# Opening, convolution end and MLP seams of a two-block transformer kernel, written in another order

## The reference, cut to what matters

```python
def first_block(x, ...):
    h = rmsnorm(x, norm1_g)
    u = h @ cc_w_in + cc_b_in                      # 2048 -> 4096
    val, gate = split(u)
    u = val * sigmoid(gate)
    u = causal_dwconv(u, cc_dw) + cc_dw_b          # 31 taps for each channel
    u = silu(layernorm(u, cc_ln_g, cc_ln_b))
    x = x + u @ cc_w_out + cc_b_out
    x = x + square(relu(rmsnorm(x, norm2_g) @ mlp_w1)) @ mlp_w2    # 2048 -> 8192 -> 2048
    return rmsnorm(x, final_g)

def second_block(x, ...):
    proj = x @ w_in                                # then pooling, sparse attention, w_out, layer norm
    ...                                            # then 128 chosen experts for each token, layer norm
```

## Time and profile before

| | |
|---|---|
| time, median of 3 runs | 2882.6 us (2881.51 to 2890.96) |
| the profiled execution: its time | 2899.03 us |
| its span, first to last instruction | 2897.1 us |
| PE busy | 2207.9 us, 76% |
| DVE busy | 1942.5 us, 67% |
| POOL busy | 2035.0 us, 70% |
| ACT busy | 1161.9 us, 40% |
| PE's mean granted clock | 0.874 of full |

### The profile page before, as it was taken

One profiled execution on the slowest core, in us unless ns is written; L12 is line 12 of the kernel. 1 busy time (PEld: TensorE's weight loads), 2 busy tenths in 40 slices (PEclk: granted clock), 3 DMA queues, 4 the chain that ended last, 5 costly groups with the idle time before them and its releaser, 6 DMA issues. The chain is left out here.

```text
span 2897.1 us, 40891 instructions
## 1 busy us (share of the span) xinstructions
PE 2207.9 (76%) x12632; PEld 1946.7 (67%) x12632; DVE 1942.5 (67%) x3016; ACT 1161.9 (40%) x1888; POOL 2035.0 (70%) x1140
## 2 busy tenths in 40 slices
PE   6998999999999999999989700002330289999996
PEld 5997788888888888999978600002220278878785
DVE  2997322624426223464445999999999888888888
ACT  4343545454454544333430100008970254444443
POOL 3773688888888877577751566787878537777774
PEclk9999999999999999999999955555555699999998
DMA  5552455555555555364434999999999649999997
GB/s 182 168 173 87 145 189 181 189 181 190 187 188 183 179 172 186 117 204 147 159 132 149 416 368 381 392 413 377 410 409 401 242 159 337 329 321 326 317 317 253
DMA packets 231978, 713.75 MB, mean 246 GB/s; under 512 B 17418, under 2 KB 53826, under 8 KB 198722
## 3 DMA queue, kind: packets, MB, share of 16 engines
q1 hardware_dynamic: 168512, 364.08, 37.3%
q0 software_dynamic: 57344, 343.97, 30.5%
q10 hardware_dynamic: 6048, 4.81, 0.5%
HBM read 709.12 MB, written 3.67 MB: 246 GB/s over the span
## 5 line engine op out<-in xcount | busy, mean ns | idle before, releaser
L381 POOL TENSOR_TENSOR w_lo<-raw,w_hi 128x1024 fp32r<-128x1024 f32 x464 | 1125.5, 2443 | 368.1 <-ACT w_hi L815 366.4
L815 ACT CAST w_hi<-raw 128x1024 fp32r<-128x1024 f32 x464 | 482.9, 1050 | 671.8 <-PE bank L460 411.1
L458 PE MATMUL bank<-B,w_hi 128*128 128x512 f32 x1280 | 457.4, 402 | 15.4 <-DVE B L1210 8.7
L458 PE MATMUL bank<-A,w_hi 128*128 128x512 f32 x1280 | 452.7, 399 | 0.0
L421 POOL DMA_INDIRECT vrows<-in_peer_v,vring x256 | 327.0, 1277 | 146.7 <-POOL vring L415 104.3
L1330 DVE TENSOR_TENSOR sq<-bank,T 128x256 f32<-128x256 f32 x128 | 54.2, 425 | 459.3 <-ACT T L942 458.9
L460 PE MATMUL bank<-B,w_lo 128*128 128x256 f32 x1280 | 361.3, 282 | 0.0
L460 PE MATMUL bank<-A,w_lo 128*128 128x256 f32 x1280 | 359.5, 281 | 0.0
L397 POOL DMA_INDIRECT rows_split<-in_peer_u,ering x128 | 253.3, 1979 | 134.5 <-DVE dots L1573 82.1
L463 PE MATMUL bank<-A,w_hi 128*128 128x256 f32 x1152 | 333.3, 289 | 5.6 <-DVE proj L1374 2.9
L464 PE MATMUL bank<-A,w_hi 128*128 128x256 f32 x1152 | 329.8, 286 | 0.0
(11 more groups left out here) (243 smaller groups left out, 4529.6 us busy)
## 6 DMA issues: line engine op xcount, KB each, us to landing
raw<-in_mlp_w SPq DMA_DIRECT2D x128, 1024.0 KB, 5.1
v_raw<-in_peer_v SPq DMA_DIRECT2D x128, 736.0 KB, 6.3
raw<-in_w_in SPq DMA_DIRECT2D x40, 1024.0 KB, 5.0
raw<-in_cc_w_in SPq DMA_DIRECT2D x64, 512.0 KB, 4.8
raw<-in_cc_w_out SPq DMA_DIRECT2D x16, 1024.0 KB, 5.0
raw<-in_w_out SPq DMA_DIRECT2D x16, 1024.0 KB, 5.1
raw<-in_peer_wq SPq DMA_DIRECT2D x16, 1024.0 KB, 5.1
vrows<-in_peer_v,vring POOLq DMA_INDIRECT x256, 6.2
```

Of the source, the lines that this page charges most:

```text
L381: nc.gpsimd.tensor_tensor(w_lo[:, s % 4], raw[:, s // 2, 2 * (s % 2):2 * (s % 2) + 2, :], w_hi[:, s % 4].bitcast(F32), ALU.subtract).then_ ...
L458: nc.tensor.matmul(bank[m][:].rearrange("p (s t) -> p s t", s=2), wh, both[:, :, kt, :], start=(kt == 0), stop=False)
L815: nc.scalar.copy(w_hi[:, s % 4], raw[:, s // 2, 2 * (s % 2):2 * (s % 2) + 2, :]).then_inc(hi_done, 1)
```

## The change

Six edits, none of which changes what is computed:

1. The depthwise taps are fetched as 124 rows of 512 numbers instead of 31 rows of 2048, to another place, so that VectorE's clearing of `dwn` goes. TensorE turns them with 4 instead of 16 instructions.
2. The squares of x are divided: ScalarE takes tokens 0 to 127 and VectorE tokens 128 to 255 by `tensor_tensor_reduce`. `xsc` is made in four halves.
3. TensorE turns x itself first, as it arrives, into eight PSUM banks, and ScalarE copies `X` right after `VT`. The turns of `xsc` come behind it. ScalarE's cast of step 2 of group 0 comes after two `A_hi` instead of before all.
4. In the last convolution group the diagonals are written between the casts, and the sigmoids stand right behind the casts.
5. One-column activations (`load_table`) load a function table ahead of its use at six places.
6. In `G_OUT` and in the MLP's last four groups ScalarE casts steps 3 to 6 of the next group before its RMS tiles (`four_more`). The mean of squares ahead of the second layer is made before step 7 instead of step 5.

```diff
-        dwn = at("dwn", o_x, [32, D])
+        dwn = at("dwn", o_z + 56 * KB, [P, D // 4])
...
@@ block.tensor
             def turn_taps():
...
-                for k in range(KT):
-                    last = nc.tensor.transpose(misc[3][:, 32 * k:32 * k + 32], dwn[:, k * P:(k + 1) * P], ident[0:32, 0:32])
+                for b in range(4):
+                    last = nc.tensor.transpose(misc[3][:, 4 * TAPS * b:4 * TAPS * (b + 1)], dwn[0:4 * TAPS, b * P:(b + 1) * P],
+                                               ident[0:4 * TAPS, 0:4 * TAPS])
...
-            pe.wait_ge(xsc_ok, 2)
-            to_channels(xsc, x_ps, n_out["rms1"], 2)
+            for r in range(KT // 2):
+                pe.wait_ge(part_in[r // 2], 16)
+                if r == 7:
+                    pe.wait_ge(vt_ok, 1)
+                to_channels(xnat, r, x_banks[r])
+            for r in range(KT // 2):
+                pe.wait_ge(xsc_ok, 2 if r < 4 else 4)
+                if r < 4:
+                    pe.wait_ge(x_ok, r + 1)
+                else:
+                    pe.wait_ge(n_out["rms1"], 2 * (r - 3))
+                to_channels(xsc, r, misc[r % 4])
...
             groups(A_hi, A_lo, G_IN, 1, n_op["rms1"], order=swap, hooks={6: turn_taps})
             pe.wait_ge(vt_ok, 2)
-            to_channels(xnat, x_ps, x_ok, 1)
...
-            project(0, {5: lambda: mean_of_sum(ssq_ok, 2 * KT, n_mean["rms3"])})
+            project(0, {7: lambda: mean_of_sum(ssq_ok, 2 * KT, n_mean["rms3"])})
@@ block.scalar
-            act.dma_start(dwn[0:TAPS, :], a["cc_dw"][0]).then_inc(rows_in, 16)
+            act.dma_start(dwn[0:4 * TAPS, :], a["cc_dw"][0].rearrange("j (c n) -> (j c) n", c=4)).then_inc(rows_in, 16)
+
+            def load_table(function, n):
+
+                nc.scalar.activation(warm[:, n:n + 1], warm[:, 7:8], function)
...
-            for s in range(3):
+            for r in range(8):
+                act.wait_ge(x_ps, r + 1)
+                nc.scalar.copy(X[:, 2 * r:2 * r + 2, :], x_banks[r][:].rearrange("p (k t) -> p k t", k=2)).then_inc(x_ok, 1)
+            for s in range(2):
                 round_sub(0, s, 32)
             for r in range(8):
+                if r == 2:
+                    round_sub(0, 2, 32)
                 act.wait_ge(n_out["rms1"], 2 * r + 2)
                 nc.scalar.copy(A_hi[:, 2 * r:2 * r + 2, :], T[:, 2 * r:2 * r + 2, :]).then_inc(n_hi["rms1"], 1)
...
-            ahead(7, 8 * 32, landed(8))
-            tap_diagonals(7, range(PE_TAPS, LAST_TAPS))
-            gates(7)
+            for s in range(3, SUBS):
+                round_sub(7, s, 8 * 32)
+                if s == 3:
+                    act.wait_ge(taps_ps, 14)
+                tap_diagonals(7, range(LAST_TAPS)[(s - 3) * LAST_TAPS // 5:(s - 2) * LAST_TAPS // 5])
+            for s in range(3):
+                round_sub(8, s, landed(8))
+            sigmoids(7)
...
+            MORE = 7
+
+            def four_more(G):
+
+                for s in range(3, MORE):
+                    round_sub(G, s, landed(G))
+
             for g in range(4):
-                ahead(G_OUT + g, landed(G_OUT + g), landed(G_OUT + g + 1))
+                G = G_OUT + g
+                ahead(G, landed(G), landed(G + 1), first=MORE if g else 3)
+                four_more(G + 1)
                 rms_tiles("rms2", g, 0)
...
             for g in range(4):
                 G = G_MLP + 28 + g
-                ahead(G, landed(G), landed(G + 1))
+                ahead(G, landed(G), landed(G + 1), first=MORE if g else 3)
                 fold_banks(G)
+                four_more(G + 1)
                 rms_tiles("rms3", g, KT)
...
+            load_table(ACT.Sqrt, 5)
             act.wait_ge(piece_used, 2 * PIECES + KEYS * PIECES)
@@ block.vector
-            V.memset(dwn[:], 0.0).then_inc(pads_xeps_ok, 1)
+            V.memset(warm[:], 1.0).then_inc(warm_xeps_ok, 1)
...
+            for c in range(4):
+                dve.wait_ge(part_in[c], 16)
+                x1 = xnat[:, 1, 512 * c:512 * c + 512]
+                V.tensor_tensor_reduce(out=T[:, 8 + 2 * c:10 + 2 * c, :].rearrange("p k n -> p (k n)"), in0=x1, in1=x1, scale=1.0,
+                                       scalar=0.0, op0=ALU.mult, op1=ALU.add, accum_out=xstat[:, 1, c:c + 1]
+                                       ).then_inc(xsq_ok, 1)
...
-            for t in range(NT):
-                V.tensor_scalar(xsc[:, t, :], xnat[:, t, :], xstat[:, t, 7:8], None, ALU.mult).then_inc(xsc_ok, 1)
+            for half in range(2):
+                cols = slice(half * D // 2, (half + 1) * D // 2)
+                for t in range(NT):
+                    V.tensor_scalar(xsc[:, t, cols], xnat[:, t, cols], xstat[:, t, 7:8], None, ALU.mult).then_inc(xsc_ok, 1)
```

More of the change, by code:

```diff
@@ L108, in build @@
         rb = at("rb", o, [BUCKETS, HEADS]); o += 64
+        warm = at("warm", o, [P, 8]); o += 64
         assert o <= nc.sbuf_usable_end, (o, nc.sbuf_usable_end)
@@ L497, in turn_taps, with to_channels @@
                 pe.wait_ge(rows_in, 32)
-                pe.wait_ge(pads_xeps_ok, 1)
                 pe.wait_ge(n_out["rms1"], KT)
-                for k in range(KT):
-                    last = nc.tensor.transpose(misc[3][:, 32 * k:32 * k + 32], dwn[:, k * P:(k + 1) * P], ident[0:32, 0:32])
+                for b in range(4):
+                    last = nc.tensor.transpose(misc[3][:, 4 * TAPS * b:4 * TAPS * (b + 1)], dwn[0:4 * TAPS, b * P:(b + 1) * P],
+                                               ident[0:4 * TAPS, 0:4 * TAPS])
                 last.then_inc(vt_ps, 1)
-            def to_channels(src, done, free, per):
-                for r in range(KT // 2):
-                    if r >= 4:
-                        pe.wait_ge(free, per * (r - 3))
-                    for i in range(4):
-                        k, t = 2 * r + i // 2, i % 2
-                        last = nc.tensor.transpose(misc[r % 4][:, i * P:(i + 1) * P], src[:, t, k * P:(k + 1) * P], ident)
-                    last.then_inc(done, 1)
-            pe.wait_ge(xsc_ok, 2)
-            to_channels(xsc, x_ps, n_out["rms1"], 2)
+            def to_channels(src, r, dst):
+                for i in range(4):
+                    k, t = 2 * r + i // 2, i % 2
+                    last = nc.tensor.transpose(dst[:, i * P:(i + 1) * P], src[:, t, k * P:(k + 1) * P], ident)
+                last.then_inc(x_ps, 1)
+            for r in range(KT // 2):
[10 more added lines that the diff above has]
+                to_channels(xsc, r, misc[r % 4])
+            pe.wait_ge(x_ok, 8)
             pe.wait_ge(vt_ok, 1)
@@ L815, in round_sub, with ahead @@
                 nc.scalar.copy(w_hi[:, s % 4], raw[:, s // 2, 2 * (s % 2):2 * (s % 2) + 2, :]).then_inc(hi_done, 1)
-            def ahead(G, now, then, last=False, middle=None):
-                for s in range(3, SUBS):
+            def ahead(G, now, then, last=False, middle=None, first=3):
+                for s in range(first, SUBS):
                     round_sub(G, s, now)
@@ L884, in tap_diagonals, with sigmoids @@
                                              ).then_inc(diag_ok, 1)
-            def gates(g):
+            def sigmoids(g):
                 for i in range(2):
@@ L892, in gates @@
                                          bias=VT[:, bass.ds(V_BG + i + 2 * g, 1)]).then_inc(bank_free[i], 1)
+            def gates(g):
+                sigmoids(g)
                 if not (isinstance(g, int) and g == 0):
@@ L905, in _ @@
             gates(0)
-            for r in range(8):
-                act.wait_ge(x_ps, r + 9)
-                nc.scalar.copy(X[:, 2 * r:2 * r + 2, :], misc[r % 4][:].rearrange("p (k t) -> p k t", k=2)
-                               ).then_inc(x_ok, 1)
             for h in range(HEADS):
@@ L926, in _ @@
             take_root("lnc")
+            load_table(ACT.Silu, 2)
             for p in range(4):
@@ L946, in mlp_in @@
                     G = q * 8 + (G_MLP + g)
-                    ahead(G, landed(G), landed(G + 1))
+                    ahead(G, landed(G), landed(G + 1), first=MORE if isinstance(q, int) and q == 0 and g == 0 else 3)
                     fold_banks(G)
@@ L1041, in _ @@
                 G = G_PROJ + i
-                ahead(G, landed(G), landed(G + 1), middle=middles.get(i))
+                ahead(G, landed(G), landed(G + 1), middle=middles.get(i), first=3 if i else MORE)
                 if i in after:
@@ L1154, in _ @@
             soft(1)
+            load_table(ACT.Gelu, 4)
             act.wait_ge(keyT_ps, 2)
@@ L1259, in _ @@
             for r in range(8):
-                dve.wait_ge(x_ps, r + 1)
+                dve.wait_ge(x_ps, r + 9)
                 for i in range(2):
```

27 lines of the change are left out of this document (15 added, 12 removed).

## The result

| | before | changed |
|---|---|---|
| median of the paired runs | 2893.65 us (13 runs, 2881.51 to 2906.79) | 2879.72 us (13 runs, 2865.8 to 2887.77) |
| ratio of the times, 95% interval | | 0.9945 (0.9923 to 0.9967) |
| profiled execution: time, span | 2899.03, 2897.1 us | 2879.8, 2877.8 us |

By the ratio the changed kernel is 16 us faster (9.5 to 22 by the interval; the two medians differ by 13.9). The forecast was 35.7 us. Part of the distance to the predicted 2847 is its base: the three runs shown had a median of 2882.6, and 13 runs have 2893.65. The rest, some 20 us, is the forecast's own.

What follows compares the result with a forecast made beforehand. TensorE was taken as the bound, with time to win only at its waits or half clock. Opening 18.0, convolution's end 5.7 and seams 12.0 sum to 35.7 us, taking a median of 2882.6 to 2847 us, range 2837 to 2860.

Steps and rivals of the forecast that it cites:

- seams: At four group changes of the MLP, waits for `w_lo` and half-clock stretches behind two would go: 12.0 us, bounds 8.6 to 12.5.
- VectorE ends at +13; it is wanted again at +22.6: At the MLP seams, with RMS tiles at +9.5 us, VectorE would still finish in time, with 9 us of slack.
- `G_OUT`, put at 0: In `G_OUT` the same move of casts ahead of the RMS tiles finds no wait to remove: gain 0.
- rival 3: At the seams, later RMS tiles hold VectorE or the rings; only half the 12 us arrives: 2853 us, 12%.
- Opening, 18.0 forecast: From the start through group 1: 9.8 to group 0, 5.5 for turning x, 2.7 for bias rows and clock; bounds 13 and 23.
- the 9.8 to group 0: In the opening, step 3 of group 0 would start at 34.9 instead of 43.9 (9.0 us); fewer tap turns give 0.8.
- 2.2 stood: Bias rows behind group 0: the clock would fall midway through them, so they take 7.0 instead of 9.2 us.
- rival 1: The clock stays up through the bias rows and group 1, gaining 4 to 4.5 us more: 2842.5 us, 12%.
- Rival 2: In the opening, the taps still hold one DMA engine and step 3 is 4 us later: 2851 us, 10%.
- about 3 us: In the opening, time for fetching the taps as 124 rows, against 11 us if all go through one engine.
- Convolution's end, 5.7 forecast: In the last convolution group, sigmoids right behind the casts let VectorE start 3.7 us earlier; gain 5.7, bounds 3.7 and 6.
- Table loads, 0: Preloading the table at the end gains 0, hidden behind VectorE's statistics; the others lie in waits.
- the opening's 3.5: In the opening, ScalarE loses four squares and a 1.28 us table load and gains a one-column activation: 3.5 us.

Runs made afterwards that it cites:

- without early steps: The changed kernel with `four_more` taken out of all `G_OUT` and MLP groups and the mean of squares back at step 5: 2873.19 us, ratio to before 0.9933.
- the PSUM edit: The changed kernel with VectorE's norm sums and products in the last MLP groups put in PSUM bank `misc` instead of `sq`: 2871.06 us, ratio to before 0.992.

## Why the prediction was wrong

The term for the **seams** failed, in the step "VectorE ends at +13; it is wanted again at +22.6". That +13 holds only with VectorE's durations from rows in which GpSimd stood idle (0.35 to 0.42 us), and the edit is just what ends that idleness. Operations that met a `w_lo` took up to 2.6. Of the forecast 12.0 us the stretch behind group 40 kept 0.7 (mean 251.8 us of the seven profiles with early steps and `sq` in SBUF, 252.5 of the three without either), and nothing if only profiles with 540.9 us for groups 17 to 40 are compared (252.7 for 252.5). `G_OUT`, put at 0, lost 4.3.

The slack of 9 us was also held against the wrong waiter. At the seam shown above (the last bank is copied at 1049.35) VectorE is done at 1067.8, some +19, and its next operation comes at 1071.84: the next banks were never late. What was late is ScalarE's cast of step 7, which stands behind the tiles. It came at 1066.82, 9 us behind the cast of step 6 where steps are 2.83 apart.

And the larger loss lies behind the seams. Counted on TensorE (from group to group, by the start of its last product with `w_lo`), groups 41 to 45 took 127.9 and 129.1 us in the two profiles of before, 128.1 without early steps, and 120.5, 120.4 and 120.0 in the three of the changed kernel: some 8 of the 12.0 us did arrive. Then TensorE has to wait for sixteen VectorE operations, `X<-X,VT,rstd` with two inputs in SBUF, before it can make its products with `X`. Their groups, before and changed, in the same views as the rows of the theory:

```profile
L1411 DVE SCALAR_TENSOR_TENSOR X<-X,VT,rstd 128x256 f32<-128x256 f32 x12 | 14.8, 1303 | 0.3 <-DVE proj L1374 0.3
```

```profile
L1456 DVE SCALAR_TENSOR_TENSOR X<-X,VT,rstd 128x256 f32<-128x256 f32 x6 | 15.4, 2627 | 0.3 <-DVE proj L1419 0.3
```

In 15 us twelve of them were made before, and six now, because GpSimd, held up at the last seam, then makes one `w_lo` after the other. All sixteen take 25.8 to 26.2 us for 20.7. TensorE waits 3.8 to 4.2 us for them in the three profiles (nothing before), and behind the wait its products with `X` ran 17.6 to 20.8 us at a mean granted clock of 0.66 to 0.79, for 16 us at 0.86 and 0.87 before. With the PSUM edit and early steps, groups 41 to 45 take 116.7 to 118.0 us, the wait is 1.4, and the products 15.4 to 16.6. The prediction has no term for these sixteen operations.

This is rival 3, against which the prediction held "9 us of slack at +13", the same number; it came out harder than its price: nothing was left instead of half. With the operands in PSUM the last stretch gives 9.5 to 10.3 us against before, near the 12.0: the reading of the waits was right, the cover was not there. That the place of the operands is the cause is shown by experiment; how the loss divides between the seams and the products with `X` is read from the traces.

The trace of before had the price. VectorE and GpSimd in its opening:

```profile
28.80 2.42 DVE L1256 TENSOR_TENSOR A<-T,A 128x512 fp32r<-128x512 f32 x1 [5.00 <-ACT A L876]
...
31.93 0.68 DVE L1256 TENSOR_TENSOR A<-T,A 128x512 fp32r<-128x512 f32 x1
```

```profile
28.32 2.34 POOL L381 TENSOR_TENSOR w_lo<-raw,w_hi 128x1024 fp32r<-128x1024 f32 x1 [5.26 <-ACT w_hi L815]
```

The same operation takes 2.42 us beside GpSimd and 0.68 alone. The MLP's first three quarters had it too: there `X<-sq,X` took 2.11 us in the mean of 48. So had the row of `xsc` that the forecast carried over as "4.57 us, same work": of its two operations of equal size the first took 1.29 us and the second, beside a `w_lo`, 3.37. In the changed kernel all of `xsc` takes 2.74, because it now comes ahead of the first `w_lo`.

**Opening, 18.0 forecast.** By the end of group 7 it is 14.9 to 16.7 us, mean 15.7 (two profiles of before, 243.1 and 242.0; three of the changed kernel, 226.4 to 227.1). Bias rows start 12.0 to 13.3 us earlier, not 15.3: the 9.8 to group 0 was too high by some 3, since three of the `A_lo` met GpSimd. And the clock: I expected it to fall inside the bias rows. In the first profile they ran at full clock and took 5.48 us; in the other two the mean granted clock over them was 0.85 and 0.82, and they took 6.3 and 6.5. Before, they took 9.20 and 8.35. So the mean gain is 2.7 where 2.2 stood: the first profile is rival 1's, the other two are the forecast's. The Trainium skill's page "TensorE: Matmul & The Clock Gate", section "🎯 Why this matters for your kernels", asks only for no idle gaps; the first profile agrees with it, and the 0.85 and 0.82 of the others, like the 0.58 of before, don't. Rival 2 falls: the 124 rows took 5.9 us, with 2.7 under way at a time, where one engine would have taken 11 by the forecast and took 13.0 for the 31 rows. The "about 3 us" was too low by half, and it cost nothing, since the wait is gone.

**Convolution's end, 5.7 forecast**: 4.2 measured, within its bounds (3.7 to 6). **Table loads, 0**: nothing that shows, but 1.28 us of the opening's 3.5 was credited to one, and group 7 ended no later without it.

**Sum.** `G_OUT` starts 20.6 us earlier (means of two and three profiles) where 23.7 was said; less 4.3, plus 0.7: 17.0. The paired runs say 16 and, the second time, 19. The base put the predicted time another 11 us too low, and one execution of a kernel alone moves by 10 between the two paces of the MLP. It was luck that `G_OUT` lost no more than 1.9 us in the first profile.

**Open.** Why TensorE runs the MLP at one or the other pace; why the PSUM edit pays 5.9 us without early steps, of which only part is accounted for (the two profiles also ran at different paces, 540.9 and 530.9); and why the time from TensorE's last value product to the last instruction is 20.3 us in both profiles of before and 21.2 to 23.4 in the three of the changed kernel.

## What to carry to other kernels

When an edit fills an engine's idle time, the durations of the other engines in that stretch are no longer those of the trace: look for a row where both are busy, and price the stretch by it. VectorE operations with two SBUF inputs beside GpSimd's subtractions cost up to a whole GpSimd instruction each here; let one operand or an intermediate result live in PSUM. Follow the engine that ends the stretch: by GpSimd's `w_lo` the seams had hardly gained, by TensorE's products they had gained 8 us, and these were lost a group later. And a few profiles of the same kernel, compared stretch by stretch, told 2 us apart here where medians of 6 to 14 runs didn't.

## What was not expected of the hardware

TensorE, busy without gap at full clock, works the same products at one of two paces that differ by 1.9% (399 or 394 ns mean for the `w_hi` product): 540.9 or 530.8 us for 24 groups. The pace can change inside an execution (22.2 us a group for 13 to 15, then 22.6 from 17 on). Bias rows that use 32 of 128 rows ran 5.5 us at full clock in one profile when they followed group 0 directly, and at a mean of 0.85 and 0.82 in two others, where before they had followed turns and waits and ran at 0.58 and 0.64.
